# Router of a mixture-of-experts block: raw tiles turned, logits by token tile, tokens gathered in turned form

## Chip, cores and metric

One Trainium2 chip, one NeuronCore of it, one launch. The metric is the device time of a run in microseconds (us). Its engines: PE (TensorE, matmuls; PEld are its weight loads), DVE (VectorE), ACT (ScalarE), POOL (GpSimd), SP (SyncE, here the queue that issues nearly all transfers).

## What is computed

Two transformer blocks in float32 over 512 tokens of width 1024. The first is attention and a SwiGLU layer, the second a gated linear attention (GLA) and a mixture of 64 experts (MoE) with a router in two steps. All that the change touches is the MoE; cut to it:

```python
h = rmsnorm(x, ffn_norm_2)                       # 512 x 1024
g_logits, e_logits = h @ w_group, h @ w_expert   # 8 groups, 64 experts
g_sel = argmax(g_logits); g_w = softmax(g_logits)[g_sel]
top_p, top_i = top_k(softmax(e_logits of the 8 experts of g_sel), 2)
gates = g_w * top_p / sum(top_p)
for each expert e, over the tokens that chose it:
    y = (silu(h @ w1[e]) * (h @ w3[e])) @ w2[e]   # 1024 -> 256 -> 1024
    x[token] += gate * y
out = rmsnorm(x, final_norm_2)
```

## The kernel before

It is a hand-written program: one instruction stream for each engine, with semaphores between them; the order of every stream is that of the code, no planner moves anything. SP's stream issues the weight transfers, each after a wait on the semaphore that says that its slot was read for the last time. Names: `T` = 4 token tiles of 128, `KD` = 8 slices of the width, `C` = 32 places of an expert, `BUNCH` = 4 experts whose 4 x 32 places fill 128 rows (`R`), `BUNCHES` = 16, `E_SLOTS` = 6 slots of gate and up weights (2 MB an expert), `D_SLOTS` = 5 slots of down weights (1 MB).

Before the MoE, `out_projection(3)` writes the GLA's result to eight PSUM banks and DVE's `residual(24, moe_input)` adds it to `xres`, tile by tile. ACT sums the squares (`squares`, L722), POOL takes the root (`root`, L2263), DVE writes the normed tile `xn` with the gain row (L1990).

The router then goes: `transposes(4)` on PE (L1072) turns all of `xn` into banks 0 to 7; ACT and DVE copy four banks each to `hT` (L729, L1996); PE multiplies with the router weights `rtw` as stationary, 72 rows by 512 tokens (L1484); DVE copies (L2015), PE turns back (L1488), DVE copies (L2017). DVE finds the best group and the two best experts of each token (L2020 to L2038) and makes one-hots `oh` and their sum `ohs` (L2040, L2042). PE forms how many tokens before each one chose the same expert: a product with a strictly triangular matrix inside a tile, and with ones over running sums `ohc` for tiles before (L1492, L1494), and the counts of each expert (L1495). From these DVE derives, in `L2060` to `L2078`, a number `val` for each token and choice: block times 32 plus rank. An expert with over 32 tokens gets extra blocks, handled by a loop at the very end that doesn't run unless there are some; `ovf_i` holds its count and its experts (L2107 to L2111, `s_tabs`).

A bunch of four experts needs: `choices` (DVE, L2084), the 0/1 matrices `E0` and `E1` of 128 tokens by 128 places for each tile and choice; `gate_column` (PE, L1502), the gate of each place, copied by DVE (L2098), which then adds `E1` to `E0` (L2099); `tokens` (PE, L1509), two halves of 512 columns, with `E0` as stationary and `xn` as moving: the 128 places' tokens as rows; ACT copies them to `G` (L968); `xT` (PE, L1517), eight transposes of `G`, each of columns 8 apart, copied by ACT to `xeT` (L973); `placesT` (L1523), four transposes of `E0` for the way back.

For each expert PE then gives `gate_up` (L1535, 64 instructions in four column groups), ACT `silu` (L985), DVE the product `hid` (L2120), PE `hidden` (L1549, turns it), DVE `hT_out` (L2140), PE `down` (L1563), ACT and DVE copy the result (L991, L2126). Results of a bunch go back to tokens by `bunch_by_token` (L1583, L1584) and are added by DVE (L2159). PE's stream for the first experts reads:

```python
gate_column(0); tokens(0, 0); tokens(0, 1); xT(0, 0, 5); xT(0, 1, 7); placesT(6)
# b = 0: expert_in(0), gate_column(1), tokens(1, 0), hidden_of(0)
# b = 1: expert_in(1), tokens(1, 1), expert_out(0), hidden_of(1)
# b = 2: expert_in(2), placesT(5), expert_out(1), hidden_of(2)
```

Here `expert_in` is `gate_up` and `expert_out(b)` is `down`. SP's stream in this place:

```python
sp.wait_ge(s_rt, 1)                      # logits done
for e in range(2, 5): down_in(e, e)      # L662
for e in range(D_SLOTS, EXPERTS):
    if e + 1 < EXPERTS:                  # L656, after gate_up of expert e - 5
        gate_up_in(e + 1, (e + 1) % E_SLOTS, e + 2 - E_SLOTS)
    down_in(e, e % D_SLOTS, e + 1 - D_SLOTS)   # after down of expert e - 5
```

At the kernel's start, ACT issues the loads of all gain vectors as rows (L706); one transpose makes columns of them (L1097).

Of the kernel before, what the change touches and what calls it, by code (L numbers as in the profile page):

```python
# [13 lines left out]
P = 128  # L14
# [34 lines left out]
def program(nc, x, meta_tokens, attn_norm, ffn_norm, final_norm, fox_w_in, fox_b_f, fox_q_norm, fox_k_norm,  # L49
# [32 lines left out]
    with ExitStack() as ctx:  # L82
# [32 lines left out]
        NGAIN = 3 * KD + GH + 2  # L115
        gcol = sb("gcol", NGAIN)
        gcols, bgate = gcol[:, 0:3 * KD], gcol[:, 3 * KD:3 * KD + GH]
        qgain, kgain = gcol[:, NGAIN - 2:NGAIN - 1], gcol[:, NGAIN - 1:NGAIN]
# [166 lines left out]
        s_rt = sem("router_logits")  # L285
        s_rte = sem("router_exp")
        s_lgT = sem("router_logitsT_out")
        s_lg = sem("router_logits_by_token")
        s_oh = sem("one_hots_ready")
        s_pre = sem("prefix_ready")  # L290
        s_tabs = sem("extra_blocks_counted")
# [8 lines left out]
        s_Ge = sem("tokens_out")  # L300
        s_xTp = sem("moe_xT")
# [265 lines left out]
        xeT = arena[:, 3712:3712 + KD * R].rearrange("p (k r) -> p k r", k=KD)  # L567
        G = arena[:, 4736:4736 + D]
        E0, E1 = (fixed[:, i * T * R:(i + 1) * T * R].rearrange("p (t r) -> p t r", t=T) for i in range(2))
# [11 lines left out]
        lgT = arena[0:NR, 4800:4800 + SEQ]  # L581
# [4 lines left out]
        pre = rpart(T * EXPERTS, T)  # L586
# [13 lines left out]
        ohc = arena[:, 4480:4480 + (T + 1) * EXPERTS]  # L600
# [6 lines left out]
        def _(sp):  # L607
# [69 lines left out]
            sp.wait_ge(s_rt, 1)  # L677
# [22 lines left out]
        def _(act):  # L700
# [23 lines left out]
            def tp_out(n, gain):  # L724
                for k in range(KD) if n < 4 else range(0, KD, 2):
# [3 lines left out]
                    act.activation(hTh[k] if n < 4 else hT[:, k, :], bank(k), ACT.Copy,  # L729
                                   scale=gain[:, k:k + 1] if gain is not None else 1.0).then_inc(s_tpA, 1)  # L730
# [224 lines left out]
            tp_out(4, None)  # L955
# [9 lines left out]
            def tokens_out(g, n):  # L965

                act.wait_ge(s_G, g * 2 + n + 1)
                act.copy(G[:, n * 512:(n + 1) * 512], bank(n)).then_inc(s_Ge, 1)  # L968

            def xT_out(g, i, b):  # L970

                act.wait_ge(s_xTp, g * 2 + i + 1)
                act.copy(xeT[:, 4 * i:4 * i + 4, :].rearrange("p k r -> p (k r)"), bank(b)).then_inc(s_xT, 1)  # L973
# [40 lines left out]

            tokens_out(0, 0)
            tokens_out(0, 1)
            xT_out(0, 0, 5)
            xT_out(0, 1, 7)
            placesT_out(0, 0, 6)
            act.wait_ge(s_tabs, 1)  # L1020
            n_over = act.value_load(ovf_i[0:1, SPILL:SPILL + 1], min_val=0, max_val=SPILL)
            for b in range(EXPERTS):
# [3 lines left out]
                if r == 0:  # L1026
                    if more:
                        tokens_out(g + 1, 0)
                    if b:
                        y_of(b - 1)  # L1030
                        bunch_high(g - 1)
                elif r == 1:
                    if more:
                        tokens_out(g + 1, 1)
                    y_of(b - 1)
                elif r == 2:
                    if more:
# [3 lines left out]
                else:  # L1041
                    if more:
                        xT_out(g + 1, 0, 5)
                    y_of(b - 1)
                    if more:
                        xT_out(g + 1, 1, 5)
            y_of(EXPERTS - 1)
            bunch_high(BUNCHES - 1)
            with act.If(n_over > 0):
                with act.Fori(0, n_over) as i:  # L1050
                    tokens_out(i + BUNCHES, 0)
                    tokens_out(i + BUNCHES, 1)
                    placesT_out(i + BUNCHES, BUNCHES % 3, 5)
                    xT_out(i + BUNCHES, 0, 5)
                    xT_out(i + BUNCHES, 1, 5)
# [9 lines left out]
        def _(pe):  # L1065
# [30 lines left out]
            pe.wait_ge(s_gin, 16 * 8)  # L1096
# [379 lines left out]
            transposes(4, lambda t: (s_hnrow, t + 1), 32)  # L1476
            pe.wait_ge(s_rtw, 32)
            w = rtw
            for k in range(KD):
                if k % 2:  # L1480
                    pe.wait_ge(s_tpD, KD * 4 + 1 + (k + 1) // 2)
                else:
                    pe.wait_ge(s_tpA, KD * 4 + k // 2 + 1)
                last = pe.matmul(bank(0)[0:NR, :], w[:, k, :], hT[:, k, :], start=(k == 0), stop=(k == KD - 1))  # L1484
            last.then_inc(s_rt, 1)
            pe.wait_ge(s_lgT, 1)
            for t in range(T):
                last = pe.transpose(bank(1)[:, t * NR:(t + 1) * NR], lgT[:, t * P:(t + 1) * P], ident[0:NR, 0:NR])  # L1488
            last.then_inc(s_lg, 1)
            pe.wait_ge(s_oh, 2)  # L1490
            n = T * EXPERTS
            pe.matmul(bank(1)[:, 0:n], strict[:, :], ohs.rearrange("p t n -> p (t n)"), start=True, stop=False)  # L1492
            pe.wait_ge(s_oh, 3)
            pe.matmul(bank(1)[:, 0:n], ones[:, :], ohc[:, 0:n], start=False, stop=True)  # L1494
            pe.matmul(bank(1)[:, n:n + EXPERTS], ones[:, :], ohc[:, n:n + EXPERTS], start=True, stop=True).then_inc(s_pre, 1)  # L1495
            def gate_column(g):

                pe.wait_ge(s_E, g + 1)
                for k, e in enumerate((E0, E1)):
                    for t in range(T):  # L1500
                        a = k * T + t
# [900 lines left out]
```

## Time and profile before

| | |
|---|---|
| median of 3 runs | 1517.52 us (1517.29 to 1517.57) |
| the profiled execution, its own time | 1517.73 us |
| its span in the trace | 1516.0 us |
| busy share of the span | PE 94%, PEld 71%, DVE 35%, ACT 35%, POOL 31% |
| DMA queue of SP | 283.60 MB, 48.2% of 16 engines |
| HBM | 188 GB/s over the span |
| POOL, 128x512 low half of a weight (L475) | 1.309 us each |
| mean granted clock of PE | 0.966 |

The span begins with the first and ends with the last instruction in the trace; the time holds 1.7 us more. Times in rows are us from the span's start. The MoE takes from about 988 us to the end. PEclk is the share of full speed that PE was granted: 1.00 is 2.4 GHz, 0.50 is 1.2 GHz. A float32 matmul of the program shows as two instructions, a transpose as one; a matmul's end is modelled and holds a drain of some 0.2 us that overlaps the next one. "idle before <-releaser" in brackets is how long the engine sat and what ended it.

### The profile page before, as it was taken

To read this page: it belongs to the slowest core of one execution; us is meant where nothing else is said; L and a number is where in the kernel's file an instruction comes from. 1 tells how busy PE (TensorE), PEld (TensorE's weight loads), DVE (VectorE), ACT (ScalarE), POOL (GpSimd) and SP (SyncE) were. 2 spreads that over 40 slices of the span, in tenths; PEclk is the share of its full clock that TensorE was granted. 3 is DMA by queue.
4 is the path that set the end of the run, shared out by engine and by line. 5 is a ranking of instruction groups with operands and counts; after the bars stand their busy time and mean duration, and the time that the engine had idled before them with its cause. 6 is when DMAs were issued, how large, how long until landed. Compare 5 with 4: busy or idle time off the path is not lost. (4 is left out here: it accounts for less than half of the span.)

```text
span 1516.0 us, 27429 instructions
## 1 busy us (share of the span) xinstructions
PE 1421.8 (94%) x11430; PEld 1070.9 (71%) x11430; DVE 531.6 (35%) x1356; ACT 523.4 (35%) x1115; POOL 474.5 (31%) x455
## 2 busy tenths in 40 slices
PE   7999999989999999999899997959999999999985
PEld 6788876667888888888677885835666666666653
DVE  3103037742222101111406315163445445445435
ACT  4325447753322222222445432212222232222222
POOL 5334545534544444444437742400000000000000
PEclk9999999989999999999899998979999999999997
DMA  5223220113133223322233222553999999999994
GB/s 179 82 87 111 84 83 32 45 57 111 59 109 111 80 87 111 111 70 70 73 112 112 77 90 73 212 209 139 421 420 419 420 420 419 419 419 419 420 420 168
DMA packets 83740, 286.51 MB, mean 189 GB/s; under 512 B 8740, under 2 KB 31424, under 8 KB 59040
## 3 DMA queue, kind: packets, MB, share of 16 engines
q1 hardware_dynamic: 83232, 283.60, 48.2%
q8 instruction: 93, 1.52, 0.4%
q0 software_dynamic: 288, 1.05, 0.2%
q14 instruction: 31, 0.25, 0.1%
q10 hardware_dynamic: 96, 0.08, 0.0%
HBM read 282.58 MB, written 2.13 MB: 188 GB/s over the span
## 5 line engine op out<-in xcount | busy, mean ns | idle before, releaser
L475 POOL TENSOR_TENSOR wring_halves<-wring,wring_halves 128x512 fp32r<-128x512 f32 x274 | 357.6, 1309 | 392.0 <-ACT wring_halves L470 391.3
L470 ACT CAST wring_halves<-wring 128x512 fp32r<-128x512 f32 x274 | 168.4, 621 | 442.5 <-PE ps L1084 426.8
L1082 PE MATMUL ps<-wring_halves,big_halves 128*128 128x512 f32 x612 | 241.5, 395 | 4.2 <-POOL wring_halves L475 2.7
L1082 PE MATMUL ps<-hT_halves,wring_halves 128*128 128x512 f32 x480 | 188.2, 392 | 1.7 <-DVE big_halves L1702 1.7
L2263 POOL TENSOR_TENSOR rstd<-rstd,half 128x1 f32<-128x1 f32 (+1 forms) x25 | 15.1, 606 | 554.4 <-DVE rstd L2216 514.4
L1083 PE MATMUL ps<-big_halves,wring_halves 128*128 128x512 f32 x480 | 187.5, 391 | 0.0
L1084 PE MATMUL ps<-hT_halves,wring_halves 128*128 128x512 f32 x480 | 187.4, 390 | 0.0
L1083 PE MATMUL ps<-wring_halves,hT_halves 128*128 128x512 f32 x436 | 171.0, 392 | 0.0
L1084 PE MATMUL ps<-wring_halves,hT_halves 128*128 128x512 f32 x436 | 170.7, 391 | 0.0
L1082 PEld LDWEIGHTS ps<-wring_halves,big_halves 128*128 128x128 f32 x612 | 115.5, 189 | 32.4 <-POOL wring_halves L475 5.3
L1509 PE MATMUL ps<-xn,fixed 128*128 128x512 f32 x256 | 122.7, 624 | 1.8 <-DVE fixed L2099 1.8
L1082 PEld LDWEIGHTS ps<-hT_halves,wring_halves 128*128 128x128 f32 x480 | 90.6, 189 | 22.1 <-POOL wring_halves L475 2.3
L1083 PEld LDWEIGHTS ps<-big_halves,wring_halves 128*128 128x128 f32 x480 | 90.5, 189 | 19.0 <-issue 0.2
L1084 PEld LDWEIGHTS ps<-hT_halves,wring_halves 128*128 128x128 f32 x480 | 90.5, 189 | 18.9
L2126 DVE COPY arena<-ps 32x256 f32<-32x256 f32 x128 | 54.4, 425 | 119.2 <-PE ps L1563 114.5
L1084 PEld LDWEIGHTS ps<-wring_halves,hT_halves 128*128 128x128 f32 x436 | 82.5, 189 | 17.6
L1083 PEld LDWEIGHTS ps<-wring_halves,hT_halves 128*128 128x128 f32 x436 | 82.6, 189 | 16.6
L2159 DVE TENSOR_TENSOR xres<-xres,ps 128x512 f32<-128x512 f32 x128 | 82.6, 684 | 21.7 <-PE ps L1584 20.9
L1509 PEld LDWEIGHTS ps<-xn,fixed 128*128 128x128 f32 x256 | 48.1, 198 | 57.8 <-issue 55.8
L1883 DVE TENSOR_TENSOR arena<-arena,ps 128x512 f32<-128x512 f32 x22 | 15.1, 684 | 195.3 <-ACT arena L878 195.3
L1862 DVE TENSOR_TENSOR xres<-xres,ps 128x512 f32<-128x512 f32 x32 | 21.9, 687 | 166.5 <-PE ps L1084 166.4
L1535 PE MATMUL ps<-big,arena 128*32 128x128 f32 x2048 | 70.8, 292 | 6.4 <-DMA big<-in_moe_w_dram 6.4
(332 smaller groups left out, 2079.0 us busy)
## 6 DMA issues: line engine op xcount, KB each, us to landing
big<-in_moe_w_dram SPq DMA_DIRECT2D x90, 1024.0 KB, 24.5
wring<-in_moe_w_dram SPq DMA_DIRECT2D x70, 1024.0 KB, 24.7
wring<-in_ffn_w_in_dram SPq DMA_DIRECT2D x22, 1024.0 KB, 6.7
hT<-in_moe_w_dram SPq DMA_DIRECT2D x20, 1024.0 KB, 25.4
wring<-in_fox_w_in_dram SPq DMA_DIRECT2D x7, 2048.0 KB, 8.4
wring<-in_gla_w_in_dram SPq DMA_DIRECT2D x6, 2048.0 KB, 8.2
mkv<-in_moe_w_dram SPq DMA_DIRECT2D x12, 1024.0 KB, 23.7
wring<-in_ffn_w_out_dram SPq DMA_DIRECT2D x4, 2048.0 KB, 7.8
```

What stands on the lines that cost most here:

```text
L470: act.copy(hi, src).then_inc(s_hi, 1)
L475: pool.tensor_tensor(lo, src, hi, ALU.subtract).then_inc(s_lo, 1)
L1082: pe.matmul(out, lhs[1], rhs[0], start=start, stop=False)
L1083: pe.matmul(out, lhs[0], rhs[1], start=False, stop=False)
L1084: return pe.matmul(out, lhs[0], rhs[0], start=False, stop=stop)
L1509: last = pe.matmul(bank(n), E0[:, t, :], xn[:, t, n * 512:(n + 1) * 512], start=(t == 0), stop=(t == T - 1))
L1535: last = pe.matmul(o[i * C:(i + 1) * C, 0:2 * HG], xeT[:, k, r * C:(r + 1) * C], w[:, :, i // 2, :, i % 2], start=(k == 0), stop=(k == KD ...
L1862: dve.tensor_tensor(d, d, bank(4 * (j ^ swap) + t), ALU.add).then_inc(s_res, 1)
L1883: dve.tensor_tensor(prod[f % 2], sg[f % 2], bank((2 * f + 1) % 8), ALU.mult).then_inc(s_hid, 1)
L2126: last = dve.tensor_copy(rows[:, n * YG:(n + 1) * YG], bank(6 + j % 2)[n * C:(n + 1) * C, 0:YG])
L2159: dve.tensor_tensor(d, d, bank(n), ALU.add).then_inc(done, 1)
L2263: rooted.inc(pool.tensor_tensor(v, v, half[0:v.shape[0], 0:v.shape[1]], ALU.pow))
```

## The change

Turning. PE turns the residual tile `xres` itself, without norm, tile by tile (`turned`), two banks a tile; ACT copies all of it. The gain is multiplied into the router weights by POOL (`s_rtg`), the root into the logits by DVE. Logits are made for each tile with the turned tile as stationary and 72 columns moving, so they come out by token and are not turned back. The fourth tile's normed row is written by DVE only after the one-hots.

Sums. The sums over tiles before are four products with `ones` or the triangle over shrinking column ranges of `ohs`, with no running sums on DVE; counts go to a bank of their own and are copied by ACT.

Places. `val` holds the place in the first 64 blocks, or a number beyond all of them where the rank is 32 or more. What concerns extra blocks (DVE from `blocks_before` to `s_tabs`) stands after the first bunch's choices.

Gather. `M` is the sum of both choices, made by the second comparison of each tile; the gate column uses `E0` times the difference of the gates plus `M` times the second. `tokens_of` has slices of `xn` (columns 8 apart) as stationary and `M` as moving, so the tokens come out turned, in the layout of `xeT`; `G`, its copies and `xT` are gone. `xeT` has two buffers. In the first bunch PE starts with each tile as its `M` is ready; gate_column(0) stands behind gate_up(0), tokens(1, 0) behind gate_up(1), tokens(1, 1) and gate_column(1) behind gate_up(2).

One gain vector more is loaded at the start by ACT's queue.

```diff
@@ SP
-            sp.wait_ge(s_rt, 1)
+            sp.wait_ge(s_lg, T)
@@ ACT, start
-            for v, n in ((attn_norm, KD), (ffn_norm, KD), (attn_norm_2, KD), (gla_b_gate, GH)):
+            for v, n in ((attn_norm, KD), (ffn_norm, KD), (attn_norm_2, KD), (gla_b_gate, GH), (ffn_norm_2, KD)):
@@ ACT, router
-            tp_out(4, None)
+            for t in range(T):
+                for i in range(2):
+                    act.wait_ge(s_tt, 2 * t + i + 1)
+                    act.copy(hT[:, 4 * i:4 * i + 4, t * P:(t + 1) * P], bank(t % 2 * 2 + i).rearrange("p (k s) -> p k s", k=4)).then_inc(s_tc, 1)
...
+            act.wait_ge(s_cnt, 1)
+            act.copy(cnt, bank(7)[:, 0:EXPERTS]).then_inc(s_cntc, 1)
...
-            xT_out(0, 0, 5)
-            xT_out(0, 1, 7)
             placesT_out(0, 0, 6)
@@ PE
+            def turned(t):
+                pe.wait_ge(s_res, 28 + t + 1)
+                for i in range(2):
+                    wait(pe, s_tc, 2 * (t - 2) + i + 1)
+                    for q in range(4):
+                        k = 4 * i + q
+                        last = pe.transpose(bank(t % 2 * 2 + i)[:, q * P:(q + 1) * P], xres[:, t, k * P:(k + 1) * P], ident[:, :])
+                    last.then_inc(s_tt, 1)
+            def logits(t):
+                for k in range(KD):
+                    if k % 4 == 0:
+                        pe.wait_ge(s_tc, 2 * t + k // 4 + 1)
+                    last = pe.matmul(bank(4 + t)[:, 0:NR], hT[:, k, t * P:(t + 1) * P], rtw[:, k, :], start=(k == 0), stop=(k == KD - 1))
+                last.then_inc(s_lg, 1)
+            turned(0)
+            pe.wait_ge(s_rtg, 1)
+            for t in range(1, T):
+                turned(t)
+                logits(t - 1)
+            logits(T - 1)
+            pe.wait_ge(s_oh, 2)
+            pe.matmul(bank(6)[:, 0:n], strict[:, :], ohs.rearrange("p t n -> p (t n)"), start=True, stop=False, skip_group_check=True)
+            for s in range(1, T):
+                last = pe.matmul(bank(6)[:, s * EXPERTS:n], ones[:, :], ohs[:, 0:T - s, :].rearrange("p t n -> p (t n)"),
+                                 start=False, stop=(s == T - 1), skip_group_check=True)
+            last.then_inc(s_pre, 1)
             for t in range(T):
+                last = pe.matmul(bank(7)[:, 0:EXPERTS], ones[:, :], ohs[:, t, :], start=(t == 0), stop=(t == T - 1))
+            last.then_inc(s_cnt, 1)
...
+            def tokens_of(t, n):
+                v = xn[:, t, :].rearrange("p (m k) -> p k m", k=KD)
+                for q in range(4):
+                    last = pe.matmul(bank(n)[:, q * R:(q + 1) * R], v[:, 4 * n + q, :], M[:, t, :], start=(t == 0 and q == 0), stop=(t == T - 1 and q == 3),
+                                     skip_group_check=True)
+                return last
...
-            gate_column(0)
-            tokens(0, 0)
-            tokens(0, 1)
-            xT(0, 0, 5)
-            xT(0, 1, 7)
+            pe.wait_ge(s_hnrow, T)
+            for t in range(T):
+                pe.wait_ge(s_M, t + 1)
+                for n in range(2):
+                    last = tokens_of(t, n)
+                    if t == T - 1:
+                        last.then_inc(s_G, 1)
             placesT(6)
@@ DVE
+            for t in range(T):
+                if t == T - 1:
+                    dve.wait_ge(s_pw, roots.n)
+                dve.wait_ge(s_lg, t + 1)
+                me.inc(dve.tensor_scalar(lg[:, t, :], bank(4 + t)[:, 0:NR], rstd[:, t:t + 1], None, ALU.mult))
...
+            moe_row(T - 1)
...
+            for k in range(2):
+                me.inc(dve.tensor_tensor(ohp[:, k * T:(k + 1) * T, :], oh[k], bank(6)[:, 0:T * EXPERTS].rearrange("p (t n) -> p t n", t=T), ALU.mult))
+            me.wait()
+            me.link(dve.tensor_reduce(rk, ohp, AX, ALU.add))
+            me.inc(dve.tensor_scalar(q1, rk, C - 0.5, 2.0 * C * EXPERTS, ALU.is_ge, ALU.mult))
+            me.inc(dve.scalar_tensor_tensor(out=val, in0=esel, scalar=float(C), in1=rk, op0=ALU.mult, op1=ALU.add))
+            me.wait()
+            me.link(dve.tensor_tensor(val, val, q1, ALU.add))
...
+                def second(t):
+                    dve.wait_ge(s_E, g * T + t + 1)
+                    dve.scalar_tensor_tensor(out=M[:, t, :], in0=place, scalar=v[:, T + t:T + t + 1], in1=E0[:, t, :],
+                                             op0=ALU.is_equal, op1=ALU.add).then_inc(s_M, 1)
...
@@ POOL
+            pool.wait_ge(s_rtw, 32)
+            pool.wait_ge(s_gain, 1)
+            pool.tensor_tensor(rtw, rtw, rgain.unsqueeze(2).to_broadcast([P, KD, NR]), ALU.mult).then_inc(s_rtg, 1)
             row_roots()
```

## Rows read from the trace of the kernel before

**Rows 1.** Stretches: us, busy us by engine (instructions), PEclk, DMA share, GB/s
```profile
1009.00:1024.00 15.00, 6.28 (x23) 5.32 (x23) 9.70 (x39) 0.10 (x2) 0.00 (x0) 0.50 0.09 37
1024.00:1037.00 13.00, 12.26 (x94) 6.71 (x94) 6.43 (x14) 4.09 (x7) 0.00 (x0) 0.88 0.00 0
1037.00:1052.00 15.00, 14.08 (x118) 7.63 (x120) 1.33 (x5) 1.55 (x4) 0.00 (x0) 0.89 0.37 141
...
1060.00:1488.00 428.00, 413.60 (x5811) 272.45 (x5810) 198.76 (x514) 115.20 (x265) 0.00 (x0) 0.97 1.01 418
```

**Rows 2.** Timeline of SP's queue: start us, us, line, issue, count
```profile
988.21 0.80 SPq L656 DMA_DIRECT2D big<-in_moe_w_dram  x2
...
1001.19 0.80 SPq L662 DMA_DIRECT2D wring<-in_moe_w_dram  x2
...
1036.89 0.80 SPq L656 DMA_DIRECT2D big<-in_moe_w_dram  x2
1052.05 0.33 SPq L662 DMA_DIRECT2D big<-in_moe_w_dram  x1
```

**Rows 3.** The chain that ended last: start us, us, what
```profile
1063.35 1.96 PE ps L1535 x64
1065.30 3.63 PE ps L1509 x8
...
1084.91 0.65 PE ps L1517 x4
...
1091.17 1.96 PE ps L1535 x64
...
1461.76 26.27 DMA wring<-in_moe_w_dram
```

**Rows 4.** Timeline of PE, 1005 to 1035 us: idle before in brackets
```profile
1009.05 1.22 PE L1492 MATMUL ps<-arena,fixed 128*128 128x256 f32 x2 [6.64 <-DVE arena L2042]
...
1019.35 3.57 PE L1502 MATMUL ps<-arena,fixed 128*128 128x1 f32 x16 [7.75 <-DVE fixed L2084]
1023.84 8.72 PE L1509 MATMUL ps<-xn,fixed 128*128 128x512 f32 x16 [0.92 <-DVE fixed L2099]
```

**Rows 5.** Timeline of DVE, 1001 to 1030 us
```profile
1002.44 0.46 DVE L2017 COPY arena<-ps 128x288 f32<-128x288 f32 x1 [0.56 <-PE ps L1488]
...
1011.70 0.42 DVE L2060 COPY arena<-ps 128x256 f32<-128x256 f32 x1 [0.82 <-PE ps L1495]
...
1017.64 1.66 DVE L2084 TENSOR_SCALAR fixed<-arena 128x128 f32<-128x128 f32 x8
...
1023.70 2.21 DVE L2107 TENSOR_TENSOR arena<-arena 1x1984 f32<-1x1984 f32 x1
```

**Rows 6.** Timeline of ACT, 988 to 1036 us
```profile
988.94 1.06 ACT L722 ACTIVATE arena<-xres 128x1024 f32<-128x1024 f32 x1 [1.57 <-DVE xres L1862]
...
993.36 2.06 ACT L729 ACTIVATE wring<-ps 128x512 f32<-128x512 f32 x4 [3.26 <-PE ps L1072]
...
1035.64 1.28 ACT L985 ACT_TABLE_LOAD   x1
```

**Rows 7.** Timeline of PE, then single lines: duration ns min/median/max
```profile
859.26 1.06 PE L1412 MATMUL ps<-big 128*128 128x128 f32 x8
...
1033.24 1.16 PE L1517 MATMUL ps<-ident,arena 128*128 128x128 f32 x8 [0.68 <-ACT arena L968]
...
L1412 PEld LDWEIGHTS ps<-big x32: 190/192/192, 859.2 to 885.8; 128*128 128x128 f32 x32
L1412 PE MATMUL ps<-big x32: 275/275/275, 859.3 to 885.9; 128*128 128x128 f32 x32
...
L1517 PEld LDWEIGHTS ps<-ident,arena x128: 185/193/207, 1033.2 to 1463.2; 128*128 128x128 f32 x128
...
L1523 PEld LDWEIGHTS ps<-ident,fixed x64: 137/140/144, 1034.1 to 1454.1; 128*128 128x128 f32 x64
```

**Rows 8.** Timeline of ACT's queue at the start
```profile
2.48 0.32 ACTq L706 DMA_DIRECT2D arena<-in_gla_b_gate_dram  x1
```

More of the change, by code:

```diff
@@ L1475, in _ @@
             out_projection(3, "gwo")
[L1476 to L1485, printed above, removed]
@@ L1486, in _ @@
-            pe.wait_ge(s_lgT, 1)
-            for t in range(T):
[L1488 to L1494, printed above, removed]
@@ new lines, in logits @@
+            def logits(t):
+                for k in range(KD):
+                    if k % 4 == 0:
[8 more added lines that the diff above has]
+            logits(T - 1)
@@ L1496, in gate_column @@
+            last.then_inc(s_cnt, 1)
             def gate_column(g):
-                pe.wait_ge(s_E, g + 1)
-                for k, e in enumerate((E0, E1)):
+                pe.wait_ge(s_M, T * g + T)
+                for k, (e, v) in enumerate(((E0, dgate), (M, gates[:, T:2 * T]))):
                     for t in range(T):
-                        a = k * T + t
-                        last = pe.matmul(bank(5)[:, 0:1], e[:, t, :], gates[:, a:a + 1], start=(a == 0), stop=(a == 2 * T - 1))
+                        last = pe.matmul(bank(5)[:, 0:1], e[:, t, :], v[:, t:t + 1], start=(k + t == 0), stop=(k == 1 and t == T - 1))
@@ L1508, in tokens @@
                 for t in range(T):
-                    last = pe.matmul(bank(n), E0[:, t, :], xn[:, t, n * 512:(n + 1) * 512], start=(t == 0), stop=(t == T - 1))
+                    last = tokens_of(t, n)
                 last.then_inc(s_G, 1)
-            def xT(g, i, b):
-                pe.wait_ge(s_Ge, g * 2 + 2)
-                v = G.rearrange("p (m k) -> p k m", k=KD)
-                for k in range(4):
-                    last = pe.transpose(bank(b)[:, k * R:(k + 1) * R], v[:, 4 * i + k, :], ident[:, :])
-                last.then_inc(s_xTp, 1)
@@ L1520, in placesT, with gate_up @@
             def placesT(b):
                 for t in range(T):
-                    last = pe.transpose(bank(b)[:, t * P:(t + 1) * P], E0[:, t, :], ident[:, :])
+                    last = pe.transpose(bank(b)[:, t * P:(t + 1) * P], M[:, t, :], ident[:, :])
                 last.then_inc(s_ST, 1)
-            def gate_up(j, slot, r, ready):
+            def gate_up(j, slot, x, r, ready):
                 w13 = w13_slot(slot)
@@ L1534, in gate_up @@
                     for i in range(4):
[L1535 removed]
+                        last = pe.matmul(o[i * C:(i + 1) * C, 0:2 * HG], x[:, k, r * C:(r + 1) * C], w[:, :, i // 2, :, i % 2],
                                          start=(k == 0), stop=(k == KD - 1), skip_group_check=True)
@@ L1618, in _ @@
                 elif r == 2:
+                    if g == 0:
+                        tokens(1, 1)
+                        pe.wait_ge(s_gc, 1)
+                        gate_column(1)
                     if more:
@@ L2077, in _ @@
-            me.link(dve.tensor_tensor(bl, bl, esel, ALU.add))
-            me.link(dve.scalar_tensor_tensor(out=val, in0=bl, scalar=float(C), in1=rk, op0=ALU.mult, op1=ALU.add))
+            me.link(dve.tensor_tensor(val, val, q1, ALU.add))
             def choices(g, v):
-                for k, e in enumerate((E0, E1)):
-                    for t in range(T):
-                        last = dve.tensor_scalar(e[:, t, :], place, v[:, k * T + t:k * T + t + 1], None, ALU.is_equal)
-                last.then_inc(s_E, 1)
+                def second(t):
+                    dve.wait_ge(s_E, g * T + t + 1)
+                    dve.scalar_tensor_tensor(out=M[:, t, :], in0=place, scalar=v[:, T + t:T + t + 1], in1=E0[:, t, :],
+                                             op0=ALU.is_equal, op1=ALU.add).then_inc(s_M, 1)
+                for t in range(T):
+                    dve.tensor_scalar(E0[:, t, :], place, v[:, t:t + 1], None, ALU.is_equal).then_inc(s_E, 1)
+                    if t:
+                        second(t - 1)
+                second(T - 1)
```

189 lines of the change are left out of this document (84 added, 105 removed).

## The prediction

> **What bounds the kernel now.** I read, in this order, the stretches with their DMA rate, SP's queue, the timelines of PE, DVE and ACT around the router, and the chain that ended last. The stretches [rows 1] show two regimes. From 1060 to 1488 us the DMA engines are full, at 418 GB/s: the expert weights stream in, and nothing in the code of PE can shorten that. From 1009 to 1052 they are nearly empty: 37, 0 and 141 GB/s. Why is in SP's queue [rows 2]: every slot was filled by the transfers issued up to 1001.19; the next, for expert 6's gate and up weights, waits for expert 0's gate_up (1036.89); the one after that, down weights of expert 5, waits for expert 0's down product (1052.05). From there issues follow fast enough that the stream does not break. The chain that ended last [rows 3] ends its long part with a transfer that lands at 1488.04, and 28 us of last expert, addition and output follow. So this kernel's end is the time at which the unbroken stream starts, plus a fixed amount of bytes, plus a fixed tail. PE goes through four experts in 27.82 us in steady state (gate_ups at 1063.35 and 1091.17) [rows 3], the stream brings four (12.58 MB) in 30.0 us: PE is the faster, and it has idled only late.
>
> What counts, then, is how much earlier gate_up(0) and down(0) are done.
>
> **Logits.** Before: PE turned all tiles after the norm, then came long matmuls over all tokens, a copy, four transposes, and a second copy on DVE that ends at 1002.90 [rows 5]. Now PE turns raw tiles as soon as the out-projection ends (988.2, where SP's next issue is released [rows 2]). ACT does all eight copies alone and only after its last squares (988.94 + 1.06 and a short accumulator read, so about 990.1) [rows 6]; pitch 2.06/4 = 0.515 us. A tile's logits are 16 matmul instructions with a full stationary and 72 columns; the nearest row is 0.112 us each for 128 columns ((1.06 - 0.275)/7, L1412) [rows 7], so 1.8 us a tile, and a turned tile 8 x 0.11 = 0.9. The order on PE is logits(0) from 990.75, turned(2), logits(1), turned(3), logits(2), logits(3): 4 x 1.8 + 2 x 0.9 = 9.0, so 999.75, with drain 1000.0, and DVE's scaled copy of 72 columns ends at 1000.3. **2.6 us earlier.** SP's three down loads, now behind the last logits, go out at 1000.0 instead of 1001.19: hidden, the queue is full then and the slots are all filled by 1009 either way. POOL's scaling of the router weights (128x576) stands between its last weight half and its first root, which waits for the first residual tile: free. If that cover went, it would delay the roots by some 1.5 us (a 128x512 half takes it 1.31 on the page). POOL's gain row load moves from 993 to about 1008, where DMA is idle; its reader is the last norm.
>
> **One-hot sums.** DVE from logits to the one-hots is unchanged, 6.15 us (1002.90 to PE's start at 1009.05) [rows 4, 5], so PE starts at 1006.45. PE then gives 2 instructions each of 256, 192, 128, 64 columns. At half clock the 256-column pair takes 1.01; by columns (each instruction at least 0.213, from the 16 of the gate column in 3.57 us [rows 4]) 2.5, and 0.35 drain: 2.9 against 2.65 from 1009.05 to DVE's read at 1011.70 [rows 5]. **0.25 later**; sums at 1009.35. The last tile's norm (1.29) and the gates lie beside it on DVE.
>
> **Places.** DVE from the sums to the first choice was 5.94 us (1011.70 to 1017.64): counts, extra blocks, two 512-wide passes. Left: two products 0.85, one reduction 0.73, three small ones 0.5: 2.1. **3.85 earlier**; choices start at 1011.45.
>
> **From choices to gather.** Before: eight choices (1.66), gate column on PE (3.57 at half clock), copy, sum of one-hots, gather at 1023.84: 6.2 us. Now the gather starts with the first tile's pair, after three instructions of 0.21: 1012.1. **5.55 earlier.** The counts on PE (8 x 0.213 = 1.7, to 1011.1) end before that; DVE and ACT have them in time.
>
> **Gather and gate_up(0).** 64 instructions of 128 columns instead of 16 of 512. At full clock 64 x 0.112 = 7.2; at half, 0.213 each, 13.6. The clock was half at 1009 to 1024 and rose some 3 us into the old gather [rows 1, 4]; I take the same: 8.8, ending at 1020.95. The two copies and xT's eight transposes between gather and gate_up fall away; the copy of the second half (0.58) overlaps placesT. gate_up(0) runs 1021.5 to 1023.5, signalled 1023.75 against 1036.89. The rest, **1.4 earlier**; sum so far 2.6 - 0.25 + 3.85 + 5.55 + 1.4 = 13.15.
>
> The extra-block chain is moved here, onto DVE: at most what it took before (5.94 + two passes the size of the 2.21 of L2107 [rows 5] + 0.6, less the 2.1 above), 8.9 us, from 1013.15 to 1022. Its first waiter is hid(0), ready at 1024.2 after ACT's silu with its 1.28 table load [rows 6]: 2 us of slack.
>
> **From gate_up(0) to down(0).** Before 15.15 us, with the gate column and both halves of the second gather in between. Now gate_column(0) 1.85, hidden 0.35, gate_up(1) 1.97, tokens(1,0) 32 x 0.112 + 0.1 = 3.7 (the choices it waits for are done at 1027.7, just when gate_up(1) ends), down(0) 1.07: 9.05, so 1032.8. **6.1 earlier.** What is late next: the second restart. down(1) sits behind gate_up(2) 2.0, tokens(1,1) 3.7, gate_column(1) 1.85, DVE's copy 0.3, placesT 0.6, down 1.0: 1042.6. The transfers released at 1032.8 (3.15 MB at 418 GB/s) last 7.5 us, to 1040.3: a new gap, **2.3 later**. After it issues at 1046 and 1054.8 come before the queue is dry.
>
> **Start of the kernel.** ACT issues one more gain load ahead of its first work: 0.32 [rows 8]; nothing covers it for certain. **0.3 later.**
>
> **Sum.** 13.15 + 6.1 - 2.3 - 0.3 = 16.6 us. The profiled execution took 1517.73 for a span of 1516.0; span 1499.4, that execution 1501.1; the median of the runs shown is 0.2 lower, 1500.9.
>
> **The steady loop** must stay under 30.0 us. It loses eight transposes (0.65 for four, so 1.3 [rows 3]) and trades 2 x 3.63 for 64 x 0.112 + 0.2: 26.6. Hidden; so the removed copies and waits are worth nothing after 1055.
>
> **A rule against the change.** The turned gather loads as stationary a view of xn whose columns are 8 floats apart. The row nearest to it is L1517, transposes of the same strided view: weight load 193 ns against 140 for packed L1523, but a pitch of (1.16 - 0.275)/7 = 0.126 at most, against 0.112 for L1412 [rows 7]. None shows a strided stationary in a plain float matmul, whose packed load already takes 192. The Trainium skill, SBUF — State Buffer, section on Door 1 (the DMA port swizzle), says that each access that crosses to a new 16-byte line pays a penalty and that four floats is as far as one strides for free. By it every weight here would pay. I bound the pitch by 0.112 and, double rate, 0.213, and take 0.112, since the strided loads of L1517 overlap too.
>
> **Rivals.** (1) *Slower:* strided weight loads set the pitch p. Four experts take 26.6 + 64(p - 0.112); gate_up(63) ends at 1021.5 + 15 x 26.6 + 14 + 1024(p - 0.112), 14 being a last group without gather. With p = 0.150 that meets the stream's 1473.5; at 0.166 it is the old 1490.1; at 0.213 it is 1538, 48 us more: 1565. For: load times of 193. Against: pitch of L1517. 4%. (2) *No change:* the same with p = 0.165 (0.112 + the 53 ns that stride adds), 1517. 3%. (3) *Clock stays at half* through gather and second tokens: +4.8 and +3.3, 1509. For: long idle of PE before. Against: PE now works through the sums and waits only 1 us. 12%. (4) *Extra-block chain or ACT late:* hid(0) 2 to 4 us behind, 1504. 12%. (5) Full clock all through: gather 7.2, sums 1.5 shorter: 1497.5. 15%. The forecast proper 54%.
>
> **Numbers.** A measurement here can tell about 0.2% (3 us) from none. Range 1495 to 1509, which holds cases 3 to 5 and leaves out 1 and 2. Faster 0.93, same 0.03, slower 0.04.
>
> **What would show it.** gate_up weights of expert 6 issued at about 1024, down of expert 5 at 1033, a short DMA gap about 1041, then 418 GB/s to about 1471; last logits read at 1000; gather from 1012 with 64 instructions 0.112 apart; 27 us or less for four experts. Wrong if the pitch is above 0.13, if DVE's extra chain runs past 1024, or if the stream breaks after 1045.

## The result, and the profile after

Before: 1517.40 us (median of 4 runs, 1515.68 to 1517.57). After: 1595.59 us (4 runs, 1594.88 to 1599.98). Ratio 1.0524, interval 1.0504 to 1.0544: **78 us slower**. The forecast was 1500.9 in a range of 1495 to 1509, and wrong; the mechanism is that of rival 1, with a pitch above the bound that I had set for it. The profiled execution took 1594.88 us for a span of 1593.1.

The page, engines and costliest groups (busy us, mean ns, idle before and its releaser):

```profile
PE 1521.8 (96%) x12124; PEld 1252.1 (79%) x12124; DVE 521.7 (33%) x1335; ACT 507.4 (32%) x1088; POOL 475.6 (30%) x456
...
PE 39%; DVE 2%; issue 1%; POOL 0%; ACT 0%; DVEq 0%; POOLq 0%; ACTq 0%
...
L1519 PE MATMUL ps<-fixed,xn 128*128 128x128 f32 x1024 | 253.3, 406 | 1.4 <-DVE fixed L2078 1.4
L1519 PEld LDWEIGHTS ps<-fixed,xn 128*128 128x128 f32 x1024 | 247.5, 336 | 7.8 <-issue 7.8
```

Two things are to be seen. The chain that ended last has no DMA in it any more, where that of before closed its long part with a transfer [rows 3]. And L1519, the turned gather, has a weight load of 336 ns and fills PEld for as long as PE: 247.5 us beside 253.3. Its stretches (us, busy us by engine with instructions in brackets, PEclk, DMA share, GB/s), against [rows 1]:

```profile
1009.00:1024.00 15.00, 14.51 (x61) 14.54 (x61) 9.60 (x26) 0.59 (x1) 0.00 (x0) 0.80 0.00 0
1120.00:1560.00 440.00, 439.22 (x5560) 371.31 (x5554) 172.01 (x444) 86.06 (x206) 0.00 (x0) 1.00 0.88 357
```

In the loop PE is busy for 439.2 of 440 us at full clock, and the stream, which came at 418 GB/s before, gets 357, because SP waits for PE: over the whole run SP's waits for L1573, the down product, add up to 441 us. The chain shows the loop's step (start us, us, what), against [rows 3]:

```profile
1166.81 1.96 PE ps L1545 x64
1168.76 7.87 PE ps L1519 x32
1176.64 1.00 PE ps L1573 x16
...
1179.87 7.87 PE ps L1519 x32
...
1202.06 1.94 PE ps L1545 x62
```

Half a gather, 32 instructions, takes 7.87 us. Four experts take 1202.06 - 1166.81 = 35.25 us; 26.6 were forecast, and the stream needs 30.0. The starts of successive records of L1519 lie 0.237 to 0.242 us apart (median 0.240). That is so in the first gather as well, below: 15.58/64 = 0.243. The granted clock was half until 1015 us and full after it, and the median pitch is 0.239 before and 0.240 after. The timeline of PE around the router (start us, us, line, count, idle before in brackets), against [rows 4]:

```profile
1003.98 1.22 PE L1499 MATMUL ps<-arena,fixed 128*128 128x256 f32 x2 [6.56 <-DVE arena L2054]
...
1009.49 15.58 PE L1519 MATMUL ps<-fixed,xn 128*128 128x128 f32 x64 [1.20 <-DVE fixed L2078]
...
1025.44 2.02 PE L1545 MATMUL ps<-big,arena 128*32 128x128 f32 x64
...
1031.74 7.84 PE L1519 MATMUL ps<-fixed,xn 128*128 128x128 f32 x32 [0.18 <-DVE fixed L2078]
```

What stands ahead of the gather went as forecast: with the offset below it begins 12.1 us earlier than before. The gather itself, 15.58 us instead of 8.72 [rows 4], took back over half of that. SP's issues that restart the stream, against [rows 2], come at

```profile
986.00 0.81 SPq L656 DMA_DIRECT2D big<-in_moe_w_dram  x2
...
997.45 0.80 SPq L662 DMA_DIRECT2D wring<-in_moe_w_dram  x2
...
1027.52 0.81 SPq L656 DMA_DIRECT2D big<-in_moe_w_dram  x2
1040.64 0.33 SPq L662 DMA_DIRECT2D big<-in_moe_w_dram  x1
```

This execution had reached the end of the out-projection 2.2 us before the other (986.00 against 988.21); I compare within the router by that offset.

### The profile page after: what moved, and what is told of

Same layout as the page of the kernel before. It is cut to its first block and busy times, and to the rows that moved or that the text cites. A ratio compares the mean times of both kernels' runs of the same rounds, so it can differ in the third digit from the quotient of the medians.

```text
span 1593.1 us, 28748 instructions
## 1 busy us (share of the span) xinstructions
PE 1521.8 (96%) x12124; PEld 1252.1 (79%) x12124; DVE 521.7 (33%) x1335; ACT 507.4 (32%) x1088; POOL 475.6 (30%) x456
## 5 line engine op out<-in xcount | busy, mean ns | idle before, releaser
L1519 PE MATMUL ps<-fixed,xn 128*128 128x128 f32 x1024 | 253.3, 406 | 1.4 <-DVE fixed L2078 1.4
L1519 PEld LDWEIGHTS ps<-fixed,xn 128*128 128x128 f32 x1024 | 247.5, 336 | 7.8 <-issue 7.8
L974 ACT COPY arena<-ps 128x512 f32<-128x512 f32 x32 | 18.8, 587 | 244.3 <-PE ps L1519 244.3
L1870 DVE TENSOR_TENSOR xres<-xres,ps 128x512 f32<-128x512 f32 x32 | 21.9, 688 | 166.4 <-PE ps L1081 166.4
```

The costliest lines, as they stand in the source:

```text
L1519: last = pe.matmul(bank(n)[:, q * R:(q + 1) * R], v[:, 4 * n + q, :], M[:, t, :], start=(t == 0 and q == 0), stop=(t == T - 1 and q == 3), ...
```

## The experiments

Theory A: the weight load of a view whose columns are 8 floats apart sets the pitch, and nothing else in the change costs. Rivals: the 64 short instructions are dear whatever their view is (B); or another edit of the change, the router or the new order, costs (C). In the ratios, "before" ran on the same chip.

**1. Columns adjacent, nothing else changed.**

```diff
-                v = xn[:, t, :].rearrange("p (m k) -> p k m", k=KD)
+                v = xn[:, t, :].rearrange("p (k m) -> p k m", k=KD)
```

> The changed kernel with one view altered: the gather's stationary is 128 adjacent columns of xn (k*128 to k*128+127) instead of 128 columns 8 floats apart, so the gathered columns meet the wrong weight rows; all instructions, counts and waits are the same. Theory A (the distance between the columns of the stationary sets the gather's pitch): pitch of L1519 0.112 us instead of 0.240, weight load 192 ns instead of 337, four experts 27 us instead of 35.25, DMA stream unbroken at 418 GB/s from about 1043, time 1500 (1496 to 1503). Theory B (plain float32 matmuls of 128 columns that move between four regions of one bank cost 0.240 whatever the view): nothing changes, 1595. Theory C (the steady loop is slow for another reason as well, the new waits or the order of the first bunch): pitch 0.112, but the time stays above 1517.

Measured: 1499.98 us (4 runs, 1497.58 to 1501.21), ratio to before 0.9892 (0.9877 to 0.9908). Its single lines (duration ns min/median/max), the stretch of the stream, its chain and SP's queue:

```profile
L1519 PEld LDWEIGHTS ps<-fixed,xn x1024: 186/192/338, 1009.1 to 1431.0; 128*128 128x128 f32 x171
L1519 PE MATMUL ps<-fixed,xn x1024: 274/275/583, 1009.1 to 1431.1; 128*128 128x128 f32 x171
```

```profile
1045.00:1460.00 415.00, 397.54 (x6265) 318.71 (x6264) 190.23 (x489) 96.33 (x230) 0.00 (x0) 0.97 1.01 419
```

```profile
1067.13 1.96 PE ps L1545 x64
...
1076.27 3.77 PE ps L1519 x32
...
1094.20 1.96 PE ps L1545 x64
```

```profile
1021.61 0.81 SPq L656 DMA_DIRECT2D big<-in_moe_w_dram  x2
1030.69 0.33 SPq L662 DMA_DIRECT2D big<-in_moe_w_dram  x1
...
1040.28 0.33 SPq L662 DMA_DIRECT2D big<-in_moe_w_dram  x1
```

One view is worth 95.6 us. The pitch (the distance from one start to the next) is 0.112 us, four experts take 27.07, under the stream's 30.0, and the stream runs at 419 GB/s again. B and C fall: the instructions are as many, and every other edit is still in.

**2 to 4. How the load grows with the distance.** Views of 2, 3 and 4 floats between columns:

```diff
-                v = xn[:, t, :].rearrange("p (m k) -> p k m", k=KD)
+                v = [xn[:, t, j * 2 * P:(j + 1) * 2 * P].rearrange("p (m k) -> p k m", k=2)[:, k, :] for j in range(KD // 2) for k in range(2)]
...
-                    last = pe.matmul(bank(n)[:, q * R:(q + 1) * R], v[:, 4 * n + q, :], M[:, t, :], start=(t == 0 and q == 0), stop=(t == T - 1 and q == 3),
+                    last = pe.matmul(bank(n)[:, q * R:(q + 1) * R], v[4 * n + q], M[:, t, :], start=(t == 0 and q == 0), stop=(t == T - 1 and q == 3),
```

Four floats is the same with 4 for 2; three floats takes `xn[:, t, j * 80:j * 80 + 3 * P - 2:3] for j in range(KD)`.

> The changed kernel with the gather's stationary columns 2 floats (8 bytes) apart; the gathered columns are in another order, so they meet the wrong weight rows. Theory A1 (a rule of 16-byte lines: free up to 4 floats): pitch 0.112, time about 1500. Theory A2 (any distance costs): pitch 0.15 to 0.24, time 1515 to 1595. Weight load between 192 and 337 ns tells how it grows.

> The changed kernel with the gather's stationary columns 4 floats (16 bytes) apart; the gathered columns are in another order, so they meet the wrong weight rows. Theory A1 (free up to 4 floats): pitch 0.112, about 1500. Theory A2 (each column its own 16-byte line costs as at 8 floats): pitch 0.24 and 1595 here, and about half of the surcharge at 2 floats.

> The changed kernel with the gather's stationary columns 3 floats (12 bytes) apart, eight overlapping views of the row: some columns are gathered twice and some not at all, and they meet the wrong weight rows. At 2 floats the pitch was 0.112 to 0.12, at 4 and 8 it was 0.24. If the price goes by the 16-byte lines touched (3 floats touch 96 lines for 128 columns, 2 floats 64, 4 floats 128): pitch about 0.18 and time 1530 to 1545. If it is a step: 0.112 and 1500, or 0.24 and 1592.

One run each, in the order 2, 4 and 3 floats: 1500.62, 1591.74 and 1532.08 us. The weight loads, now in the order 2, 3, 4 floats, one fence a kernel, and last that of the change (8 floats):

```profile
L1519 PEld LDWEIGHTS ps<-fixed,xn x1024: 193/197/336, 1011.4 to 1430.6; 128*128 128x128 f32 x171
```

```profile
L1519 PEld LDWEIGHTS ps<-fixed,xn x1024: 251/261/330, 1009.4 to 1476.6; 128*128 128x128 f32 x171
```

```profile
L1519 PEld LDWEIGHTS ps<-fixed,xn x1024: 307/329/331, 1009.6 to 1536.2; 128*128 128x128 f32 x171
```

```profile
L1519 PEld LDWEIGHTS ps<-fixed,xn x1024: 312/337/340, 1009.5 to 1539.4; 128*128 128x128 f32 x171
```

| floats between columns | 16-byte lines that hold the 128 columns | load, median ns | pitch, ns | us |
|---|---|---|---|---|
| 1 | 32 | 192 | 112 | 1499.98 |
| 2 | 64 | 197 | 118 | 1500.62 |
| 3 | 96 | 261 | 175 | 1532.08 |
| 4 | 128 | 329 | 233 | 1591.74 |
| 8 | 128 | 337 | 240 | 1595.59 |

The pitch is the median distance between the starts of two records at full clock; a line here is a stretch of 16 bytes that starts at a multiple of 16. From 2 floats on the pitch follows the lines: 233 - 175 = 58 and 175 - 118 = 57 ns for 32 lines more, 1.8 ns a line (the load itself grows by 64 and 68 ns, 2.0 to 2.1 a line); from 4 to 8 floats, no more lines, the pitch grows by 7. With one float 32 lines would make 58 ns by the same measure, and the pitch of 0.112 us that packed L1412 has [rows 7] stands instead. In these views lines and distance grow together up to four floats, and no run has a view that would part them; what tells for the lines is that the growth all but ends at four floats.

Where the granted clock was half (the first gathers, and with 2 floats a few later ones) the pitch is 213 ns with 1, 2 and 3 floats, and 233 and 239 with 4 and 8, nearly the same as at full clock. These figures fit the longer of two times, one that goes by the clock and one that goes by the view.

The experiment with 4 floats was made to tell whether four floats are free, and they are not: it costs 92 us of the change's 96. The one with 3 floats was made after these two, with its number worked out from the lines before it ran, and it fell in its range: there four experts take 31.07 us (gate_ups at 1146.77 and 1177.84), just over the stream's 30.0. The 0.6 us between 1 and 2 floats can't be told from none.

**5. The same, with the right columns.** In the four kernels so far the gathered columns do not belong to the weight rows that they meet. Here DVE writes the normed row in the gather's order, reading it 8 floats apart, and the gather's view is packed:

```diff
-                dve.scalar_tensor_tensor(out=xn[:, t, :], in0=xres[:, t, :], scalar=rstd[:, t:t + 1], in1=gainrow[:, :],
-                                         op0=ALU.mult, op1=ALU.mult).then_inc(s_hnrow, 1)
+                turn = lambda v: v.rearrange("p (m k) -> p k m", k=KD)
+                dve.scalar_tensor_tensor(out=xn[:, t, :].rearrange("p (k m) -> p k m", k=KD), in0=turn(xres[:, t, :]), scalar=rstd[:, t:t + 1],
+                                         in1=turn(gainrow[:, :]), op0=ALU.mult, op1=ALU.mult).then_inc(s_hnrow, 1)
```

> The same adjacent stationary, made right: DVE writes the normed row in the order in which the gather reads it (input and gain row read 8 floats apart, output written packed), so the output is the reference's. Theory A: as packed_view, about 1500, plus what DVE's strided read costs on the path of the first tiles (0 to 1.3 us for the last tile's row, if it takes up to twice the 1.28 us): 1499 to 1503. If DVE pays more than 2.5 us a row it delays the first gather by as much, up to 1506. Theory B: 1595.

Measured: 1506.34 us (5 runs, 1504.38 to 1508.96), ratio 0.9937 (0.9923 to 0.9951). That is 3 us above the 1499 to 1503 that I expected for rows under 2.5 us; up to 1506 was meant for longer ones. Its timeline of DVE, and below it the same row of the changed kernel:

```profile
985.77 2.14 DVE L1996 SCALAR_TENSOR_TENSOR xn<-xres,rstd,gainrow 128x1024 f32<-128x1024 f32 x1 [0.68 <-POOL rstd L2280]
987.83 0.68 DVE L1870 TENSOR_TENSOR xres<-xres,ps 128x512 f32<-128x512 f32 x1
...
1000.99 0.29 DVE L2029 TENSOR_SCALAR arena<-ps,rstd 128x72 f32<-128x72 f32 x1 [1.57 <-PE ps L1488]
```

```profile
984.71 1.29 DVE L1995 SCALAR_TENSOR_TENSOR xn<-xres,rstd,gainrow 128x1024 f32<-128x1024 f32 x1 [0.68 <-POOL rstd L2279]
986.01 0.69 DVE L1870 TENSOR_TENSOR xres<-xres,ps 128x512 f32<-128x512 f32 x1
...
997.53 0.29 DVE L2028 TENSOR_SCALAR arena<-ps,rstd 128x72 f32<-128x72 f32 x1 [1.57 <-PE ps L1488]
```

A strided row takes DVE 2.1 us instead of 1.29, and behind it in DVE's order waits the residual addition of the next tile (L1870), for which PE's turning waits: the last logits are read 19.1 us after the first row's start (982.21 here) and not 15.8 (981.98 to 997.82 in the changed kernel). That is 3.3 us of the 6.8 between the profiled executions of this kernel and of experiment 1. The out-projection ended 0.6 us later here, the places' transposes and down(1) fell into a half-clock stretch (1.3 us more), and the last gate_up and the end of the kernel met more of half clock (1.4 us); whether the change has a part in where the clock falls is not shown.

**6. The strided rows moved to where DVE waits.** On top of 5:

```diff
             def moe_input(t):
...
-                if t < T - 1:
-                    dve.wait_ge(s_pw, roots.n)
-                    moe_row(t)
...
             for t in range(T):
-                if t == T - 1:
-                    dve.wait_ge(s_pw, roots.n)
+                dve.wait_ge(s_pw, roots.n - (T - 1) + t)
+                if t < T - 1:
+                    moe_row(t)
                 dve.wait_ge(s_lg, t + 1)
```

> packed_norm with the normed rows of tiles 0 to 2 written by DVE between the logits' copies instead of between the residual's additions. Output is the reference's. Theory: packed_norm lost 6 us on packed_view because its three rows of 2.1 us (1.28 packed) hold up the residual additions and with them turning and logits (down weights' issue at 1000.9 instead of 997.1). Between the copies DVE waits 2.3 us each, which covers a row: time as packed_view, 1500 (1498 to 1502). If instead the strided read slows something else (POOL or the last row on the path of the gates) it stays near 1506.

Measured: **1497.37 us** (4 runs, 1496.90 to 1501.36), ratio to before 0.9885 (0.987 to 0.990), and 98 us under the changed kernel; three of the four runs lie below the 1498 to 1502 that I expected. DVE's timeline, PE's first gather, and SP's queue:

```profile
989.50 0.29 DVE L2027 TENSOR_SCALAR arena<-ps,rstd 128x72 f32<-128x72 f32 x1 [0.27 <-PE ps L1488]
989.71 2.10 DVE L1996 SCALAR_TENSOR_TENSOR xn<-xres,rstd,gainrow 128x1024 f32<-128x1024 f32 x1
992.12 0.29 DVE L2027 TENSOR_SCALAR arena<-ps,rstd 128x72 f32<-128x72 f32 x1 [0.31 <-PE ps L1488]
```

```profile
1008.66 7.38 PE L1519 MATMUL ps<-fixed,xn 128*128 128x128 f32 x64 [1.51 <-DVE fixed L2077]
```

```profile
1018.50 0.80 SPq L656 DMA_DIRECT2D big<-in_moe_w_dram  x2
1027.59 0.33 SPq L662 DMA_DIRECT2D big<-in_moe_w_dram  x1
```

Rows 0 to 2 now stand ahead of the copies of the logits; between two of these DVE waited 2.32 us for PE, and a row hides there: the copies follow each other at 2.61 us with it as without it. Here the clock was full in the first gather (7.38 us, against 10.02 in experiment 1), which in the profiled executions is most of the 3 us under experiment 1; why it was full here is not shown, so these 2.6 us can't be credited to the order.

**7. The gather of before, in the changed kernel.** Router and order as changed; `M` stationary and `xn` moving in two halves of 512, `G`, its copies and eight transposes back. The second half of `G` lies where the extra-block chain has its products (`ohp`), so this kernel also makes ACT wait for that chain (`s_tabs`) before the second copy; the lines below are those of the gather alone:

```diff
-                for q in range(4):
-                    last = pe.matmul(bank(n)[:, q * R:(q + 1) * R], v[:, 4 * n + q, :], M[:, t, :], start=(t == 0 and q == 0), stop=(t == T - 1 and q == 3),
-                                     skip_group_check=True)
-                return last
+                return pe.matmul(bank(n), M[:, t, :], xn[:, t, n * 512:(n + 1) * 512], start=(t == 0), stop=(t == T - 1), skip_group_check=True)
...
+            def xT(g, i, b):
+                pe.wait_ge(s_Ge, g * 2 + 2)
+                v = G.rearrange("p (m k) -> p k m", k=KD)
+                for k in range(4):
+                    last = pe.transpose(bank(b)[:, k * R:(k + 1) * R], v[:, 4 * i + k, :], ident[:, :])
+                last.then_inc(s_xTp, 1)
```

> The changed kernel with the gather of the kernel before: M as stationary, xn as moving in two halves of 512 columns, copies to G, eight turns of G (columns 8 floats apart, as before), one xeT. Router, one-hot sums, places, extra blocks behind the choices and the order of the first bunch stay as changed. Output is the reference's. Theory (all that the change gains is in the router and the order, the turned gather gives only the two copies and turns of the first bunch): four experts 27.8 us as before, stream unbroken, and 2.5 to 3.5 us later than packed_view by the copies and turns between the first gather and gate_up(0): 1503 (1501 to 1506). Rival (the gain comes from the turned gather): 1512 or more.

Measured: 1502.62 us (5 runs, 1502.16 to 1506.96), ratio 0.9919 (0.9905 to 0.9932), in the expected range. This kernel's timeline of PE, and ACT's second copy to `G`:

```profile
1009.11 7.10 PE L1532 MATMUL ps<-xn,fixed 128*128 128x512 f32 x16 [1.40 <-DVE fixed L2109]
1019.37 1.16 PE L1546 MATMUL ps<-ident,arena 128*128 128x128 f32 x8 [3.15 <-ACT arena L977]
```

```profile
1018.73 0.58 ACT L977 COPY arena<-ps 128x512 f32<-128x512 f32 x1 [2.75 <-DVE arena L2154]
```

The change splits: the router and the new order are worth 1516 - 1502.6, some 13 us. The gather in turned form costs 93 us as written (1595.59) and saves 2.6 with packed columns (1499.98). The 2.6 is not a clean price of the turned form. Of PE's wait of 3.15 us, some 2.5 come from the extra-block chain (DVE's L2154, which released ACT's copy at 1018.7; PE's gather had ended at 1016.2), and a `G` stored elsewhere would not have them. On the other side the first gather ran at full clock here (7.10 us) and at half for its first 5.6 us in experiment 1 (10.02). With both taken out some 3 us are left (2.6 - 2.5 + 2.9), an estimate that no run tests.

**8. Strided writing in place of strided reading.** Experiment 5 with the strides on the output:

```diff
-                turn = lambda v: v.rearrange("p (m k) -> p k m", k=KD)
-                dve.scalar_tensor_tensor(out=xn[:, t, :].rearrange("p (k m) -> p k m", k=KD), in0=turn(xres[:, t, :]), scalar=rstd[:, t:t + 1],
+                turn = lambda v: v.rearrange("p (k m) -> p k m", k=KD)
+                dve.scalar_tensor_tensor(out=xn[:, t, :].rearrange("p (m k) -> p k m", k=KD), in0=turn(xres[:, t, :]), scalar=rstd[:, t:t + 1],
```

> As packed_norm, but DVE reads packed and writes 8 floats apart. Output is the reference's. If a strided write costs DVE less than a strided read: rows below 2.1 us and time under 1506; at 1.28 us a row 1500. If it costs the same or more: 1506 or later.

One run: 1506.83 us; the rows take 2.0 to 2.1 us. The side on which DVE strides makes no difference that can be told.

**9. The order changed in the weights instead.** Packed view, rows of the norm as they were, and gate and up weights loaded in the order that fits:

```diff
-            W1 = moe_w1[0].rearrange("e (p k) n -> e p (k n)", k=KD)
+            W1 = moe_w1[0].rearrange("e (k p) n -> e p k n", k=KD)
...
-                    sp.dma_start(w13[:, g, :, :].rearrange("p k n -> p (k n)"), src[e]).then_inc(s_e13[j], 16)
+                    sp.dma_start(w13[:, g, :, :], src[e]).then_inc(s_e13[j], 16)
```

(`W3` likewise.)

> packed_view with the gate and up weights loaded in the matching row order (row k*128+p on partition p), so the output is the reference's and DVE writes xn packed; each partition's 8 KB piece of a transfer becomes eight of 1 KB. If small pieces cost the DMA engines nothing: 1500. The expert stream is the bound there, so each per cent it loses is 4.4 us: 1505 at 1%, over 1540 at 10%.

One run: 1557.39 us. The stretch of the stream, then the page's packets:

```profile
1045.00:1460.00 415.00, 367.19 (x5635) 294.34 (x5631) 174.54 (x454) 87.12 (x208) 0.00 (x0) 0.95 1.07 369
```

```profile
DMA packets 198449, 286.59 MB, mean 184 GB/s; under 512 B 8748, under 2 KB 162512, under 8 KB 190128
```

Two thirds of the stream's bytes, the gate and up weights, now come in pieces of 1 KB instead of 8 KB; the down weights keep theirs of 8 KB. The whole comes at 369 GB/s instead of 419, with the DMA engines full. If the down weights still came at 419, the small pieces would have come at 348, an estimate. The pitch is 0.112 us and PE has time; the stream is the bound, and it is slower. Of the three places tried, the turned order is paid cheapest on DVE.

**10. Pairs.** DVE writes the row in four instructions of 256 columns, reading pieces of 8 bytes, and the gather's view is that of 2 floats, which experiment 2 had shown to be nearly free:

```diff
+                turn = lambda v: v.rearrange("p (m j i) -> p j m i", j=KD // 2, i=2)
+                for j in range(KD // 2):
+                    last = dve.scalar_tensor_tensor(out=xn[:, t, j * 2 * P:(j + 1) * 2 * P].rearrange("p (m i) -> p m i", i=2), in0=turn(xres[:, t, :])[:, j],
+                                                    scalar=rstd[:, t:t + 1], in1=turn(gainrow[:, :])[:, j], op0=ALU.mult, op1=ALU.mult)
+                last.then_inc(s_hnrow, 1)
```

> DVE writes the normed row in pairs: columns 2j and 2j+1 of each eight side by side, in four instructions of 256 columns that read pieces of 8 bytes, 32 bytes apart; the gather reads its stationary 2 floats apart. Rows stand where the change has them, in the residual. Output is the reference's. The gather's pitch should be that of the view 2 floats apart (0.12). If DVE's price, too, is for each 16-byte line or so, a row costs less than the 2.1 us of single floats but more than 1.28: about 1.7, time 1503. If DVE pays as for single floats, 1507.

One run: 1501.93 us, 1.68 us a row for the four, both near what was expected (1503, 1.7). It lies between the medians of 5 and 6, but single runs of these spread over 4.5 us, and it was not combined with 6's order.

## Why the prediction was wrong

**The step that failed** is the pitch of the turned gather, "I bound the pitch by 0.112 and, double rate, 0.213, and take 0.112, since the strided loads of L1517 overlap too". Measured: 0.240, above the upper bound too. I had taken the price from the transposes of the same strided view, where the load takes 193 ns and the pitch is 0.126 at most [rows 7]. The plain float matmul on that view has loads of 337 ns (experiment 1: 192 when packed). A sign of the difference was in the code and the counts: the gather's 512 calls are 1024 instructions, each with its load, the 128 calls of L1517 are 128. The prediction had counted the instructions rightly, 64 in a gather, but not asked whether they load as those of L1517 do. The row with the same view was not the nearest row; the operation differed. Why a transpose's load of a strided view stays at 193 was not tried and stays open.

**The upper bound** was not a bound: 0.213 is what an instruction with a packed load takes at half clock [rows 4], and the time of the strided view does not go by the granted clock. Its pitch is 0.239 at half and 0.240 at full clock in the first gather.

**Rival 1's arithmetic** gave the result once the right p was put in: 26.6 + 64 x (0.240 - 0.112) = 34.8 us for four experts (measured 35.25), the end of gate_up(63) at 1434.5 + 1024 x 0.128 = 1565.6 (measured 1565.05 + 1.98 = 1567.0). With some 27 us of tail this is 1593, against 1594.88. It had 4% for want of a row; "With p = 0.150 that meets the stream" is borne out: a pitch of 0.118 (2 floats) costs nothing that can be told, 0.175 (3 floats) costs 32 us, where the arithmetic gives 1434.5 + 1024 x 0.063 - 1473.5 = 25.5. It is short there mainly because four experts at the packed pitch take 27.07 us and not 26.6.

**The rule set against the change** was right in kind. What the rows show: from 2 to 4 floats the pitch grows by 1.8 ns for each further 16-byte line that the load touches. The Trainium skill, SBUF — State Buffer, section on Door 1 (the DMA port swizzle), has the lines, and says that at least two accesses to a line are needed to hide the latency; the trace agrees, since 2 floats, two columns to a line, costs 118 ns against 112. Its figure of four floats as the farthest free stride does not hold here: four floats has one column to a line, and 233 ns. I had discarded the rule for the row of L1517; one doubtful row against a rule that names the mechanism deserved more than 4%.

**The other steps** held. Experiment 1 is the change as I had costed it, and came at 1499.98 where 1500.9 was forecast. That it came so close is in part luck: its out-projection had ended 2.57 us earlier than that of before, which no term of the sum holds, and with this added its profiled execution would stand at 1502.4 against 1501.1. Two of the prediction's sums do not add up as written (8.94 for the 9.05 us to down(0), 9.45 for the 9.8 from there to down(1)), and rival 5 comes to 1497.8 by its own terms, not 1497.5; each is off by less than 0.5 us. By the offset of the end of the out-projection (2.21 us for the changed kernel, 2.57 for experiment 1):

| step | forecast | measured, offset added |
|---|---|---|
| last logits read | 1000.3 | 997.82 + 2.21 = 1000.03 |
| sums begin on PE | 1006.45 | 1003.98 + 2.21 = 1006.19 |
| first choice | 1011.45 | 1008.60 + 2.21 = 1010.81 |
| gather begins | 1012.1 | 1009.49 + 2.21 = 1011.70 |
| gate_up(0) signalled (experiment 1) | 1023.75 | 1021.61 + 2.57 = 1024.18 |
| down(0) signalled | 1032.8 | 1030.69 + 2.57 = 1033.26 |
| down(1) signalled | 1042.6 | 1040.28 + 2.57 = 1042.85 |

Rival 4 did not come, though here the slow gather gave the chain more room: in the changed kernel the extra-block chain ran from 1010.49 to 1019.08 (8.6 us, 8.9 forecast), and its first waiter stood at 1027.79. Rivals 3 and 5, the clock, both came in part: the first gather took 10.02 us in experiment 1 and 7.38 in experiment 6, against the 8.8 taken. The 0.3 us for one more load at the start can't be told from these profiles. That the changed kernels ended the out-projection 0.3 to 3.1 us before the profiled execution of before (987.93 in experiment 8, 985.06 in experiment 6, against 988.21) was not forecast; the profiles differ in the length of half-clock stretches far ahead of the router, and before itself spread over 1514.2 to 1517.9 us on one chip. Whether the change has a part in it stays open.

## What to carry to other kernels

Price a new operand layout from a row that has both the same view and the same operation. Where there is no such row, no bound is known either: ask at what price the loop that is hidden now would become the bound (0.150 here), and measure the new view alone before building on it. Turning by the choice of what is stationary was free here only where the stationary's columns were adjacent or 2 floats apart; if they are not, let an idle engine lay them out once, in a place where it waits (2.1 us a tile here), rather than the load 1024 times or the DMA in small pieces. A loop with 3 us of slack in 30 went from hidden to the bound by one view.

## What the runs showed of the hardware that I had not expected

- The time of a float weight load of 128 columns grew with the 16-byte lines that they lie in: 192, 197, 261, 329 ns for 32, 64, 96, 128 lines (1, 2, 3, 4 floats apart), and 337 for 128 lines 32 bytes apart. With 4 and 8 floats the pitch was nearly the same at 1.2 and 2.4 GHz of granted clock (233 and 233, 239 and 240 ns); with 1 to 3 floats it was 213 at 1.2 GHz.
- A float32 transpose that reads its source 8 floats apart had loads of 193 ns, a plain float32 matmul whose stationary has the same distance 337 ns.
- DVE's row of 128x1024 with three operands takes 1.29 us packed, 1.68 with inputs in pairs (four instructions), 2.1 with inputs 8 floats apart, and 2.0 to 2.1 with the output 8 floats apart.
- A stream with two thirds of its bytes in pieces of 1 KB reached 369 GB/s where one with all in pieces of 8 KB reached 419, both with the DMA engines full.
